# A two-block transformer kernel on one core: identity first, flips and weights in turn, small vectors between the weights, a few products on a cleared tile

## The chip, the cores and the metric

The kernel runs on one core of a Trainium2 chip. The metric is the device time of one execution in microseconds (us). The engines are TensorE (PE in the profile, its weight loads PEld), VectorE (DVE), ScalarE (ACT), GpSimd (POOL) and SyncE (SP), which here only issues transfers. A transfer issued by SP or ACT runs on 16 DMA engines that all queues share.

## What is computed

The input x has 256 rows of 2048 numbers in fp32. A first block adds stick-breaking attention and a squared-ReLU MLP, a second block runs two layers of latent attention beside a gated depthwise convolution. Cut to what the start of the program touches:

```python
hn = rms_norm(x, norm_mix_g)
q, k, v = split(hn @ sb_w_qkv, 3)          # 2048 x 6144 weights: the first work of TensorE
q = rms_norm(q per head, q_g); k = rms_norm(k per head, k_g)
...                                         # attention, w_o, MLP of 8192
cos, sin = rope_tables(positions)           # second block
mod = silu(c) @ ada_w[l] + ada_b[l]         # shift, scale, gate
u = causal_depthwise_conv(u, dw_w[l], dw_b[l])   # 31 taps
```

## The kernel before, in words

All weights are streamed once from HBM. A **unit** is 256 rows of a weight matrix by up to 512 columns, 512 KB, and there are 648 of them. SP loads it into one of NR = 5 buffers of RAW. ScalarE rounds it to fp32r (WH, four buffers), VectorE subtracts to get the rest (WL), and TensorE then multiplies: for each of the two 128-row pieces and each half of x three products (high by high, high by low, low by high), 12 matmuls of 512 columns. A load may be issued when the unit five places earlier has left its buffer, that is when its WL is written (`w_low`).

The first eight units, 0 to 7, are the first 512 columns of the query weights and each needs two of the sixteen 128-column pieces of x turned over. That is `x_turn` i: four transposes on TensorE, two ACTIVATEs to AH on ScalarE (times the gain norm_mix_g), two subtractions to AL on VectorE. Unit i needs `x_turn` i and the x piece i // 2.

Every engine walks through the same list of steps, -1, 0, 1, ... Step n stands behind unit n on TensorE. In each step an engine first does the tasks filed under `after[n]` and then, on ScalarE and VectorE, converts the units filed under `split[n]`. Unit u is converted in step u - 4, so three units ahead of use; only the first few are earlier. Nothing is reordered: an engine that waits in its list holds all that stands behind.

```python
for i in range(3):
    after[-1].append(("x_turn", "qkv", i))
for i in range(3, 8):
    after[i - 3].append(("x_turn", "qkv", i))
...
after[6].append(("columns", 0))
```

The task `columns` turns small vectors into columns. They are gathered in VR by 14 transfers, with the convolution taps in DR (31 rows, 248 KB), the positions in PI and four copies of norm gains in TRG (`vload`, 20 transfers). SP issues these after the first five weights. On VectorE `columns` also copies the taps and computes the rotary angles, a chain of small operations. TensorE needs consts (CST, 400 KB, its first 128 columns are the identity) before it can turn anything. ACT issues that transfer, behind the gain.

Of the kernel before, what the change touches and what calls it, by code (L numbers as in the profile page):

```python
# [80 lines left out]
def build(nc, A, out):  # L81
    ctx = ExitStack()
    with ctx:
# [21 lines left out]
        FB = put("FB", [128, 4, 512])  # L105
# [73 lines left out]
        vload, col = [], {"norm_mix_g": VC[:, 0:16]}  # L179
# [12 lines left out]
        vload.append((DR[:, :, :], A["dw_w_2"].rearrange("l k c -> k l c"), {}))  # L192
        vload.append((PI[:, :], A["positions_2"].rearrange("a (t p) -> p (a t)", p=128), {"allow_slow_non_contiguous": True}))
        for l in range(2):
            vload.append((TRG[:, 2 * l, :], A["q_norm_g_2"][l:l + 1, 128:192].to_broadcast([128, 64]), {}))
            vload.append((TRG[:, 2 * l + 1, :], A["k_norm_g_2"][l:l + 1, 128:192].to_broadcast([128, 64]), {}))
# [198 lines left out]
        T = Banks(P, 4, [sem(f"bank_ready{i}") for i in range(4)], [sem(f"bank_emptied{i}") for i in range(4)])  # L395
        s_cst, s_gain, s_vec, s_bias, s_out = sem("consts_in"), sem("gain_in"), sem("vectors_in"), sem("bias_in"), sem("stored")
# [43 lines left out]
        def tensor_program(e):  # L440
# [17 lines left out]
            def columns(part):  # L458
                pb = bank(("columns", 0))
                e.wait_ge(s_vec, 16 * len(vload))  # L460
# [3 lines left out]
                m.then_inc(*T.filled(("columns", 0)))  # L464
                pb = bank(("columns", 1))
                for l in range(2):
# [165 lines left out]
            tasks = dict(x_turn=x_turn, columns=columns, ada_sum=ada_sum, qk_turn=qk_turn, sb_scores=sb_scores, sb_sums=sb_sums, sb_out=sb_out,  # L632
# [26 lines left out]
            for name, *a in after[-1]:  # L659
                if name in tasks:  # L660
                    tasks[name](*a)
# [27 lines left out]
        def scalar_program(e):  # L689
# [32 lines left out]
            def columns(part):  # L722
                e.wait_ge(*cols.at("rest"))
                e.activation(CC[:, :], col["c_2"], ACT.Silu).then_inc(*c_act.up(0))
# [260 lines left out]
            for step in range(-1, NU):  # L985
                for name, *a in after[step]:
                    if name in tasks:
                        tasks[name](*a)
                highs(step)

        def vector_program(e):
# [31 lines left out]
            def columns(part):  # L1023
# [7 lines left out]
                e.tensor_tensor(GQ[:, 1:3], col["q_norm_g_2"], col["k_norm_g_2"], ALU.mult).then_inc(*cols.up("gq"))  # L1031
                e.wait_ge(*T.ready(("columns", 1)))
                e.tensor_copy(DW[:, :, :, :].rearrange("p a b c -> p (a b c)"), T.ap(("columns", 1))[:, 0:496]).then_inc(*T.drained(("columns", 1)))
# [92 lines left out]
            def rope_tables(l):  # L1126
                e.wait_ge(*angle_a.at("cos"))
                e.wait_ge(s_vec, 16 * len(vload))
# [185 lines left out]
            tasks = dict(x_turn=x_turn, x_add=x_add, rms=rms, columns=columns, ada_sum=ada_sum, qk_norm=qk_norm, sb_scores=sb_scores, sb_sums=sb_sums,  # L1314
# [26 lines left out]

            e.wait_ge(*T.ready(("mix", 0)))
            e.tensor_copy(VC[:, 0:16], T.ap(("mix", 0))[:, 0:16]).then_inc(*T.drained(("mix", 0)))
            for step in range(-1, NU):
# [5 lines left out]
        def pool_program(e):  # L1350
# [60 lines left out]
            for step in range(-1, NU):  # L1411
# [4 lines left out]
        def sync_program(e):  # L1416
# [106 lines left out]
```

## Time and profile before

| | |
|---|---|
| runs of the kernel before, us | 1999.87, 2002.76, 2004.25 (median 2002.76) |
| the profiled execution, us | 1999.04 |
| its span, us | 1997.2 |
| granted TensorE clock, mean over the span | 0.992 |
| busy: PE, DVE, ACT, POOL | 98%, 75%, 51%, 6% |

The span is the time from the first to the last record of the profiled execution, 1.8 us less than its own time. A busy share is taken over the whole span. A matmul that waits for its operands is not busy, and one that runs at the lower clock is. The engines work side by side, so the shares don't add up.

### The profile page before, as it was taken

The page shows a single profiled execution, that of the slowest core. Times are in us where ns is not written, and L with a number is a line of the kernel's source. Part 1 is how long each engine was busy: PE and PEld are TensorE (multiplying, and loading weights), DVE is VectorE, ACT ScalarE, POOL GpSimd, SP SyncE. Part 2 cuts the span into 40 slices and gives each one's busy share as a digit, 9 for nine tenths or more (in the row PEclk, how much of TensorE's full clock was granted, in tenths as well). Part 3 has the DMA queues.
Part 4 walks back from the last instruction along what each step waited for, and adds up shares of the span by engine and source line. Part 5 has one row for each costly group of instructions (what it writes and reads, how often), then busy time and mean ns, then how long its engine had stood idle before and what let it go on. Part 6 is the DMA issues. An engine that isn't in the chain of part 4 may idle for free.

```text
span 1997.2 us, 24786 instructions
## 1 busy us (share of the span) xinstructions
PE 1950.3 (98%) x9260; PEld 1628.1 (82%) x9260; DVE 1499.6 (75%) x2013; ACT 1019.5 (51%) x1471; POOL 126.7 (6%) x86
## 2 busy tenths in 40 slices
PE   7999999999999999999999989999999899999998
PEld 5788888888888888888888878888877688888877
DVE  4787777777677777767775567988886778888865
ACT  5455455445444444453434454566645545667452
POOL 0222232000000000000000000101000000011000
PEclk9999999999999999999999999999999999999999
DMA  6776867788888888888886545654544466555444
GB/s 219 250 240 226 291 219 259 246 282 308 277 298 280 291 303 283 296 289 293 284 301 222 187 153 147 203 167 141 166 147 158 128 191 183 167 161 153 159 146 139
DMA packets 225167, 441.95 MB, mean 221 GB/s; under 512 B 15685, under 2 KB 56919, under 8 KB 225047
## 3 DMA queue, kind: packets, MB, share of 16 engines
q1 hardware_dynamic: 224867, 439.93, 68.0%
q8 instruction: 74, 1.21, 0.2%
q14 instruction: 46, 0.38, 0.1%
q10 hardware_dynamic: 180, 0.43, 0.1%
HBM read 438.20 MB, written 2.10 MB: 220 GB/s over the span
## 4 chain that ended last, share of the span: by engine, by line
PE 80%; DVE 6%; issue 6%; ACT 4%; POOL 3%; SPq 1%; DMA 1%; POOLq 0%; DVEq 0%; ACTq 0%
PE P L681 24%; PE P L683 24%; PE P L682 24%; PE P L449 2%; DVE WL L996 2%; POOL ST L1352 2%; DVE CA L993 1%; PE P L477 1%; POOL QK L1374 1%; SPq L1448 1%; ACT WH L980 1%; PE P L554 1%; DMA RAW<-in_sb_w_qkv_dram 1%; PE P L564 0%; PE P L565 0%
## 5 line engine op out<-in xcount | busy, mean ns | idle before, releaser
L996 DVE TENSOR_TENSOR WL<-RAW,WH 128x1024 fp32r<-128x1024 f32 x648 | 790.4, 1225 | 340.5 <-ACT WH L980 339.0
L980 ACT ACTIVATE WH<-RAW 128x1024 fp32r<-128x1024 f32 x648 | 670.8, 1045 | 596.2 <-PE P L683 464.8
L681 PE MATMUL P<-WH,AH 128*128 128x512 f32 (+1 forms) x1536 | 604.7, 394 | 8.1 <-DVE WL L996 5.7
L683 PE MATMUL P<-WH,AL 128*128 128x512 f32 (+1 forms) x1536 | 595.3, 388 | 0.0
L682 PE MATMUL P<-WL,AH 128*128 128x512 f32 (+1 forms) x1536 | 594.4, 387 | 0.0
L681 PE MATMUL P<-WH,BH 128*128 128x512 f32 x896 | 355.8, 397 | 0.0
L682 PE MATMUL P<-WL,BH 128*128 128x512 f32 x896 | 351.2, 392 | 0.0
L683 PE MATMUL P<-WH,BL 128*128 128x512 f32 x896 | 351.2, 392 | 0.0
L681 PEld LDWEIGHTS P<-WH,AH 128*128 128x128 f32 x1536 | 289.4, 188 | 65.9 <-issue 4.9
L683 PEld LDWEIGHTS P<-WH,AL 128*128 128x128 f32 x1536 | 289.3, 188 | 59.1
L682 PEld LDWEIGHTS P<-WL,AH 128*128 128x128 f32 x1536 | 289.7, 189 | 55.5
L993 DVE SCALAR_TENSOR_TENSOR ADA<-RAW,CC,ADA 128x1024 f32<-128x1024 f32 x180 | 238.3, 1324 | 0.0
L993 DVE SCALAR_TENSOR_TENSOR CA<-UT,DW,CA 128x256 f32<-128x256 f32 x480 | 204.3, 477 | 0.0
L683 PEld LDWEIGHTS P<-WH,BL 128*128 128x128 f32 x896 | 169.8, 189 | 36.2
L682 PEld LDWEIGHTS P<-WL,BH 128*128 128x128 f32 x896 | 169.9, 190 | 34.3
L681 PEld LDWEIGHTS P<-WH,BH 128*128 128x128 f32 x896 | 169.6, 189 | 34.1
L1352 POOL TENSOR_TENSOR ST<-ST,CST 128x4 f32<-128x4 f32 (+2 forms) x34 | 62.8, 1846 | 1584.2 <-DVE ST L1021 943.2
L1013 DVE TENSOR_TENSOR X<-X,P 128x512 f32<-128x512 f32 x72 | 46.2, 682 | 8.6 <-PE P L683 8.6
L996 DVE TENSOR_TENSOR BL<-FB,BH 128x512 fp32r<-128x512 f32 x32 | 22.2, 692 | 26.0 <-ACT BH L802 26.0
L698 ACT ACTIVATE JX<-X 128x512 f32<-128x512 f32 x32 | 20.2, 631 | 39.4 <-DVE X L1013 21.9
L798 ACT ACTIVATE FB<-P 128x512 f32<-128x512 f32 x32 | 19.2, 599 | 29.6 <-PE P L449 29.6
L996 DVE TENSOR_TENSOR BL<-P,BH 128x512 fp32r<-128x512 f32 x24 | 16.5, 688 | 20.0 <-ACT BH L964 13.9
(242 smaller groups left out, 1407.6 us busy)
## 6 DMA issues: line engine op xcount, KB each, us to landing
RAW<-in_ada_w_dram SPq DMA_DIRECT2D x192, 512.0 KB, 4.9
RAW<-in_mlp_w_in_dram SPq DMA_DIRECT2D x128, 512.0 KB, 4.5
RAW<-in_mlp_w_out_dram SPq DMA_DIRECT2D x128, 512.0 KB, 5.2
RAW<-in_sb_w_qkv_dram SPq DMA_DIRECT2D x96, 512.0 KB, 4.7
RAW<-in_w_in_dram SPq DMA_DIRECT2D x80, 512.0 KB, 3.8
RAW<-in_w_in_dram SPq DMA_DIRECT2D x128, 256.0 KB, 3.2
RAW<-in_w_out_dram SPq DMA_DIRECT2D x64, 512.0 KB, 3.7
RAW<-in_sb_w_o_dram SPq DMA_DIRECT2D x32, 512.0 KB, 5.6
```

The lines of the kernel that those rows point to most:

```text
L449: m = e.transpose(pb[:, (2 * i + t) * 128:(2 * i + t + 1) * 128], src[:, t, kt * 128:(kt + 1) * 128], IDN)
L477: m = e.matmul(pb[:, j:j + 1], ACC2[:, slot, j * 128:(j + 1) * 128], ONE[:, 0:1], start=True, stop=True)
L554: m = e.transpose(pb[0:n, (2 * h + t) * 128:(2 * h + t + 1) * 128], src, IDN)
L681: e.matmul(o, xh, wh, start=st and k == 0, stop=False)
L682: e.matmul(o, xh, wl, start=False, stop=False)
L683: m = e.matmul(o, xl, wh, start=False, stop=u.last and k == u.nk - 1)
L698: e.activation(scratch, x, ACT.Square, scale=scale, accum_out=total).then_inc(*tally.up(*name))
L980: e.activation(WH[:, n % NH, 0:size], RAW[:, i % NR, 0:size], ACT.Copy).then_inc(w_high, 1)
L993: return e.scalar_tensor_tensor(out=o, in0=x, scalar=s, in1=y, op0=op0, op1=op1)
L996: return e.tensor_tensor(o, x, h.bitcast(F32), ALU.subtract)
L1013: m = e.tensor_tensor(o, o, psum(g, c, t), ALU.add)
L1352: return e.tensor_tensor(o, x, MH.to_broadcast([128, n]), ALU.pow)
```

## The change

It does five things. (1) ACT issues the identity alone (128 columns) first, then the gain, then the other 673 columns of consts, with a semaphore for each. (2) There is a step -2: `x_turn` i moves from step i - 3 to step i - 2 (0 to -2, 1 to -1, 2 to 0), and units 0 and 1 are converted in steps -2 and -1, one behind each turn. (3) The 14 transfers to VR are issued in pairs behind loads 5 to 11, and the other six (`late`) one by one behind loads 12 to 17. (4) `columns` moves from step 6 to step 9; the taps and the angles become a task of their own, `taps`, in step 20, and ScalarE's sines move from steps 9 and 10 to steps 21 and 22. (5) VectorE clears 256 columns of FB, and TensorE runs four fp32 products on them ahead of everything else.

```diff
+        after[20].append(("taps",))
...
-            step = -1 if u < 2 else 0 if u < 4 else u - 4
+            step = u - 2 if u < 3 else max(u - 4, 0)
...
-        for i in range(3):
-            after[-1].append(("x_turn", "qkv", i))
-        for i in range(3, 8):
-            after[i - 3].append(("x_turn", "qkv", i))
+        for i in range(8):
+            after[i - 2].append(("x_turn", "qkv", i))
...
-        after[6].append(("columns", 0))
-        after[9].append(("angles", 0))
-        after[10].append(("angles", 1))
+        after[9].append(("columns",))
+        after[20].append(("taps",))
+        after[21].append(("angles", 0))
+        after[22].append(("angles", 1))
...
+            e.wait_ge(warm, 1)
+            for i in range(4):
+                e.matmul(P[:, 3, 0:256], FB[:, 0, 0:128], FB[:, 0, 0:256], start=True, stop=True)
             e.wait_ge(s_gain, 16)
-            e.wait_ge(s_cst, 16)
+            e.wait_ge(s_idn, 16)
...
+            e.dma_start(CST[:, 0:128], A["consts"][:, 0:128]).then_inc(s_idn, 16)
             e.dma_start(VR[0:16, 0, :], A["norm_mix_g"].rearrange("a (r p) -> (a r) p", p=128)).then_inc(s_gain, 16)
-            e.dma_start(CST[:, :], A["consts"]).then_inc(s_cst, 16)
+            e.dma_start(CST[:, 128:801], A["consts"][:, 128:801]).then_inc(s_cst, 16)
...
             load(4)
-            for dst, src, k in vload:
-                e.dma_start(dst, src, **k).then_inc(s_vec, 16)
             for i in range(5, len(items)):
                 load(i)
+                if i < 12:
+                    for dst, src, k in vload[2 * i - 10:2 * i - 8]:
+                        e.dma_start(dst, src, **k).then_inc(s_vec, 16)
+                elif i < 12 + len(late):
+                    dst, src, k = late[i - 12]
+                    e.dma_start(dst, src, **k).then_inc(s_late, 16)
```

ScalarE's list from the gain to unit 5, before (AH is a turned piece of x, WH a converted unit, x2 two of the same in a row, JX,ST the sums of squares):

```order
L709 ACTIVATE AH<-P,VC 128x256 x6
L980 ACTIVATE WH<-RAW 128x1024 x2
L709 ACTIVATE AH<-P,VC 128x256 x2
L980 ACTIVATE WH<-RAW 128x1024 x3
L709 ACTIVATE AH<-P,VC 128x256 x2
L980 ACTIVATE WH<-RAW 128x1024
```

and of the change:

```order
L716 ACTIVATE AH<-P,VC 128x256 x2
L987 ACTIVATE WH<-RAW 128x1024
L716 ACTIVATE AH<-P,VC 128x256 x2
L987 ACTIVATE WH<-RAW 128x1024
L716 ACTIVATE AH<-P,VC 128x256 x2
L987 ACTIVATE WH<-RAW 128x1024 x3
L716 ACTIVATE AH<-P,VC 128x256 x2
L987 ACTIVATE WH<-RAW 128x1024
```

The first unit's WH now stands behind one turned pair and no longer behind three; each later turn stands one step nearer to the unit that needs it.

SP's list behind the x pieces and weights 0 to 4, before, first and last of the 20 small transfers:

```order
L1448 DMA VR<-in_norm_mlp_g_dram 16x128
L1448 DMA VR<-in_norm_g_dram 32x128
...
L1448 DMA VR<-in_ada_b_dram 96x128
L1448 DMA DR<-in_dw_w_dram 31x2x1024
L1448 DMA PI<-in_positions_dram 128x2x1
L1448 DMA TRG<-in_q_norm_g_dram 128x64
...
L1441 DMA RAW<-in_sb_w_qkv_dram 128x2x512 x12
```

and of the change, loads 11 to 15:

```order
L1453 DMA RAW<-in_sb_w_qkv_dram 128x2x512
L1463 DMA VR<-in_c_dram 16x128
L1463 DMA VR<-in_ada_b_dram 96x128
L1453 DMA RAW<-in_sb_w_qkv_dram 128x2x512
L1466 DMA DR<-in_dw_w_dram 31x2x1024
L1453 DMA RAW<-in_sb_w_qkv_dram 128x2x512
L1466 DMA PI<-in_positions_dram 128x2x1
L1453 DMA RAW<-in_sb_w_qkv_dram 128x2x512
L1466 DMA TRG<-in_q_norm_g_dram 128x64
```

The block of small transfers that stood between loads 4 and 5 is gone; the taps now stand between loads 12 and 13.

## Rows read from the trace of the kernel before

**Rows 1.** Windows: length, then PE, PEld, DVE, ACT, POOL busy us, granted clock, DMA
```profile
200.00:1000.00 800.00, 798.50 (x3746) 665.28 (x3745) 596.59 (x570) 375.95 (x445) 44.89 (x29) 1.00 0.84 281
```
**Rows 2.** Timeline of PE: the taps' turns, starts of units 8, 9, 10, 11
```profile
41.85 1.18 PE L469 MATMUL P<-CST,DR 31*128 31x31 f32 x16
...
45.81 0.39 PE L681 MATMUL P<-WH,AH 128*128 128x512 f32 x1
...
48.53 0.39 PE L681 MATMUL P<-WH,AH 128*128 128x512 f32 x1
...
53.22 0.50 PE L681 MATMUL P<-WH,AH 128*128 128x512 f32 x1 [1.81 <-DVE WL L996]
...
57.66 0.40 PE L681 MATMUL P<-WH,AH 128*128 128x512 f32 x1
```
**Rows 3.** Timeline of PE behind unit 0: turn 3, then unit 1
```profile
19.22 0.95 PE L449 MATMUL P<-CST,X 128*128 128x128 f32 x4
19.93 0.48 PE L681 MATMUL P<-WH,AH 128*128 128x512 f32 x1
```
**Rows 4.** Timeline of the start: start us, length us, engine, line, [idle before <-releaser]
```profile
7.67 0.25 PE L658 MATMUL P<-CST,VR 16*128 16x16 f32 x1 [7.67 <-DMA CST<-in_consts_dram]
...
9.08 2.54 ACT L709 ACTIVATE AH<-P,VC 128x256 fp32r<-128x256 f32 x6 [6.07 <-PE P L449]
...
11.51 2.00 ACT L980 ACTIVATE WH<-RAW 128x1024 fp32r<-128x1024 f32 x2
...
13.96 0.76 PE L681 MATMUL P<-WH,AH 128*128 128x512 f32 x1 [3.28 <-DVE WL L996]
```
**Rows 5.** Timeline of ACT and PE: weights 5 and 6 converted, units 5 and 6 start
```profile
32.15 1.06 ACT L980 ACTIVATE WH<-RAW 128x1024 fp32r<-128x1024 f32 x1 [7.47 <-DMA RAW<-in_sb_w_qkv_dram]
...
35.21 1.04 ACT L980 ACTIVATE WH<-RAW 128x1024 fp32r<-128x1024 f32 x1
...
35.31 0.50 PE L681 MATMUL P<-WH,AH 128*128 128x512 f32 x1 [2.00 <-DVE AL L993]
...
38.35 0.50 PE L681 MATMUL P<-WH,AH 128*128 128x512 f32 x1
```
**Rows 6.** Timeline of DVE: taps copied, three steps of the angles, units 10 and 11
```profile
46.54 0.67 DVE L1033 COPY DW<-P 128x496 f32<-128x496 f32 x1
...
48.56 2.40 DVE L993 SCALAR_TENSOR_TENSOR AG<-AG 128x64 f32<-128x64 f32 x3
...
51.94 2.36 DVE L996 TENSOR_TENSOR WL<-RAW,WH 128x1024 fp32r<-128x1024 f32 x2
```
**Rows 7.** Transfers, issue to landing in us: x piece 0, weight 0, weight 4
```profile
X<-in_x_dram SPq DMA_DIRECT2D x1, 512.0 KB, 4.4
RAW<-in_sb_w_qkv_dram SPq DMA_DIRECT2D x1, 512.0 KB, 6.3
RAW<-in_sb_w_qkv_dram SPq DMA_DIRECT2D x1, 512.0 KB, 11.6
```
**Rows 8.** The chain of waits, SP's issues of the same three; then weight 5's flight
```profile
0.74 0.43 SPq L1444
1.23 0.47 SPq L1441
...
5.58 0.53 SPq L1441
...
21.15 10.98 DMA RAW<-in_sb_w_qkv_dram
```
**Rows 9.** The page: line, engine, operation, tiles, count | busy us, mean ns | idle before
```profile
L993 DVE SCALAR_TENSOR_TENSOR ADA<-RAW,CC,ADA 128x1024 f32<-128x1024 f32 x180 | 238.3, 1324 | 0.0
```
**Rows 10.** Timeline of PE: an fp32 product of 256 columns (two records), the next one
```profile
97.92 0.59 PE L493 MATMUL P<-QT 128*128 128x256 f32 x2
98.35 0.38 PE L494 MATMUL P<-QT 128*128 128x128 f32 x2
```
**Rows 11.** Windows: the queue between weight 4 and weight 5 (columns as in rows 1)
```profile
17.00:21.00 4.00, 4.00 (x15) 3.14 (x14) 0.00 (x0) 0.73 (x3) 0.00 (x0) 1.00 0.15 35
```

More of the change, by code:

```diff
@@ L191, in build @@
                 nrow[g] = r + n
[L192 to L193 removed]
+        late.append((DR[:, :, :], A["dw_w_2"].rearrange("l k c -> k l c"), {}))
+        late.append((PI[:, :], A["positions_2"].rearrange("a (t p) -> p (a t)", p=128), {"allow_slow_non_contiguous": True}))
         for l in range(2):
[L195 to L196 removed]
+            late.append((TRG[:, 2 * l, :], A["q_norm_g_2"][l:l + 1, 128:192].to_broadcast([128, 64]), {}))
+            late.append((TRG[:, 2 * l + 1, :], A["k_norm_g_2"][l:l + 1, 128:192].to_broadcast([128, 64]), {}))
         of = lambda name, n, l: col[name][:, n * l:n * l + n]
@@ L456, in x_turn, with columns @@
                 turn(pb, X, 1, 2 * i + 1).then_inc(*T.filled(("x_turn", g, i)))
-            def columns(part):
+            def columns():
                 pb = bank(("columns", 0))
+                e.wait_ge(s_cst, 16)
                 e.wait_ge(s_vec, 16 * len(vload))
@@ L464, in columns, with taps @@
                 m.then_inc(*T.filled(("columns", 0)))
+            def taps():
                 pb = bank(("columns", 1))
+                e.wait_ge(s_late, 16 * len(late))
                 for l in range(2):
@@ L630, in p_turn @@
                 turn(pb, MP, 1, 2 * i + 1).then_inc(*T.filled(("pt2", l, c, i)))
-            tasks = dict(x_turn=x_turn, columns=columns, ada_sum=ada_sum, qk_turn=qk_turn, sb_scores=sb_scores, sb_sums=sb_sums, sb_out=sb_out,
+            tasks = dict(x_turn=x_turn, columns=columns, taps=taps, ada_sum=ada_sum, qk_turn=qk_turn, sb_scores=sb_scores, sb_sums=sb_sums, sb_out=sb_out,
                          hid_turn=hid_turn, h_turn=h_turn, glu=glu, lat_turn=lat_turn, att_turn=att_turn, att_scores=att_scores,
@@ L653, in await_rows @@
                     e.wait_ge(*T.emptied(("pt2", g[1], (k - 8) // 4, k // 2 % 2)))
+            e.wait_ge(warm, 1)
+            for i in range(4):
+                e.matmul(P[:, 3, 0:256], FB[:, 0, 0:128], FB[:, 0, 0:256], start=True, stop=True)
             e.wait_ge(s_gain, 16)
-            e.wait_ge(s_cst, 16)
+            e.wait_ge(s_idn, 16)
             pb = bank(("mix", 0))
             e.transpose(pb[:, 0:16], VR[0:16, 0, :], CST[0:16, 0:16]).then_inc(*T.filled(("mix", 0)))
-            for name, *a in after[-1]:
+            for name, *a in after[-2] + after[-1]:
                 if name in tasks:
@@ L720, in x_square, with columns @@
                     square_sum(JX[:, t, :], X[:, t, c * 512:(c + 1) * 512], ST[:, 64 + 4 * t + c:65 + 4 * t + c], sq_sum, g, c, t)
-            def columns(part):
+            def columns():
                 e.wait_ge(*cols.at("rest"))
@@ L980, in highs @@
                         e.activation(WH[:, n % NH, 0:size], RAW[:, i % NR, 0:size], ACT.Copy).then_inc(w_high, 1)
+            e.dma_start(CST[:, 0:128], A["consts"][:, 0:128]).then_inc(s_idn, 16)
             e.dma_start(VR[0:16, 0, :], A["norm_mix_g"].rearrange("a (r p) -> (a r) p", p=128)).then_inc(s_gain, 16)
-            e.dma_start(CST[:, :], A["consts"]).then_inc(s_cst, 16)
+            e.dma_start(CST[:, 128:801], A["consts"][:, 128:801]).then_inc(s_cst, 16)
             e.preload_act_table_set("silu_and_others")
-            for step in range(-1, NU):
+            for step in range(-2, NU):
                 for name, *a in after[step]:
@@ L1021, in rms, with columns @@
                 e.tensor_scalar(ST[:, 72:74], ST[:, 72:74], 1.0 / D, EPS, ALU.mult, ALU.add).then_inc(*ms.up(g))
-            def columns(part):
+            def columns():
                 e.wait_ge(*T.ready(("columns", 0)))
@@ L1031, in columns, with taps @@
                 e.tensor_tensor(GQ[:, 1:3], col["q_norm_g_2"], col["k_norm_g_2"], ALU.mult).then_inc(*cols.up("gq"))
+            def taps():
                 e.wait_ge(*T.ready(("columns", 1)))
+                e.wait_ge(s_cst, 16)
                 e.tensor_copy(DW[:, :, :, :].rearrange("p a b c -> p (a b c)"), T.ap(("columns", 1))[:, 0:496]).then_inc(*T.drained(("columns", 1)))
@@ L1127, in rope_tables @@
                 e.wait_ge(*angle_a.at("cos"))
-                e.wait_ge(s_vec, 16 * len(vload))
+                e.wait_ge(s_late, 16 * len(late))
                 if l:
@@ L1312, in o_add @@
                     e.tensor_tensor(o, o, FB[:, t, :], ALU.add).then_inc(*(x_done if part else x_mid).up(l, c, t))
-            tasks = dict(x_turn=x_turn, x_add=x_add, rms=rms, columns=columns, ada_sum=ada_sum, qk_norm=qk_norm, sb_scores=sb_scores, sb_sums=sb_sums,
+            tasks = dict(x_turn=x_turn, x_add=x_add, rms=rms, columns=columns, taps=taps, ada_sum=ada_sum, qk_norm=qk_norm, sb_scores=sb_scores, sb_sums=sb_sums,
                          sb_out=sb_out, hid_turn=hid_turn, mod_scale=mod_scale, x_norm=x_norm, h_turn=h_turn, h_low=h_low_, pads=pads_, rope_tables=rope_tables,
@@ L1340, in lows @@
                             fma(acc, r, CC[:, kt:kt + 1], acc, ALU.mult, ALU.add).then_inc(ada_used, 1)
+            e.memset(FB[:, 0, 0:256], 0.0).then_inc(warm, 1)
             e.wait_ge(*T.ready(("mix", 0)))
             e.tensor_copy(VC[:, 0:16], T.ap(("mix", 0))[:, 0:16]).then_inc(*T.drained(("mix", 0)))
-            for step in range(-1, NU):
+            for step in range(-2, NU):
                 for name, *a in after[step]:
@@ L1410, in pool_program @@
             e.wait_ge(s_cst, 16)
-            for step in range(-1, NU):
+            for step in range(-2, NU):
                 for name, *a in after[step]:
```

3 lines of the change are left out of this document (2 added, 1 removed).

## The prediction, as it was put on record before the result

> **What bounds the kernel now.** I read the page first: TensorE is busy for 98% of the span, the others for 75% and less (the table above). The windows then say where its idle time lies. In a stretch of 800 us in the middle TensorE is busy 798.5 [rows 1], so a weight that arrives earlier there is worth nothing, and what TensorE lacks at the start is carried to the end: whatever brings its steady part forward by 1 us shortens the program by about 1 us. The change touches the first 22 steps only, so I followed TensorE from unit to unit up to the 12th. A unit costs 2.72 us where nothing holds it (45.81 to 48.53 [rows 2]), a turn of x 0.7 (19.22 to 19.93 [rows 3]). Against that TensorE loses five pieces:
>
> - It waits for the consts until 7.67, and unit 0 starts at 13.96 [rows 4].
> - Unit 0 takes 5.26 us (13.96 to 19.22 [rows 3, 4]), twice its price. So its matmuls stand 0.44 us apart, at 1.2 GHz, where those of unit 8 stand 0.23 apart, at 2.4 GHz: 2.5 us lost.
> - 2.0 us ahead of unit 5. TensorE waits for AL, which stands on ScalarE and VectorE behind weight 5, and ScalarE had waited 7.47 us for that transfer [rows 5].
> - 1.8 us ahead of unit 10, whose WL VectorE writes only after taps and angles: the chain runs from 46.54 to 51.94, 5.4 us [rows 2, 6].
> - Unit 10 takes 4.44 us (53.22 to 57.66 [rows 2]): the clock fell behind that pause, 1.7 us lost.
>
> **The change part by part.**
>
> *Identity first, one turn and one unit in turn.* x piece 0 is issued at 0.74 and lands 4.4 later, at 5.1; weight 0 is issued at 1.23 and lands 6.3 later, at 7.5 [rows 7, 8]. The bytes ahead of them stay the same but for the order on ACT's queue. The identity alone is not in the trace. It is 64 KB of the 400, issued 0.5 us earlier than consts were, so it can't land after consts did (7.5) and hardly after x piece 0; I take 5.1 for the first transpose. From TensorE's first product to ScalarE's first AH were 1.4 us (7.67 to 9.08), and six AH took 2.54, so two take 0.85 [rows 4]: AH 0 ends at 5.1 + 1.4 + 0.85 = 7.4. Then WH 0 can start when weight 0 is there, 7.5, where it was 11.51. From WH 0 to unit 0 were 2.45 us [rows 4]; unit 0 starts at about 9.95, **4.0 us earlier**. Bounds: if the identity came no earlier than consts, WH 0 would start at 9.9, and 2.4 of the 4.0 would go; nothing lets unit 0 start before weight 0 has landed, so there is no gain beyond 4.0 but the few tenths by which that landing may move. Turn 2, done before unit 0 until now, comes behind it: **0.7 us later**. Does one unit of lead suffice for a turn? ScalarE's round of AH, two sums of squares and WH takes 3.06 us (32.15 to 35.21 [rows 5]), a unit with its turn 3.4 on TensorE, and AL is needed a full unit after the transposes. So it does; in the first steps WH 3 and WH 4 wait for weight 4 (5.58 + 11.6 = 17.2 [rows 7, 8]) ahead of turn 3, and I find 0 to 0.3 us for unit 3.
>
> *Small vectors behind the loads.* Weight 5 was issued at 21.15 and landed 10.98 later, at 32.13 [rows 8], although its buffer was free once WL 0 was written, before unit 0 began at 13.96 [rows 4]. Now it is issued at about 9.9, directly behind weight 4, and lands about 1.2 us behind 17.2 (eight transfers of this size landed from 7.5 to 17.2). ScalarE no longer waits for it, and the pause ahead of unit 5 goes: **2.0 us**.
>
> *Taps and angles in step 20.* The 16 turns of the taps (1.1 us on TensorE) are only moved. VectorE has only the copies of the small vectors in step 9, so the pause ahead of unit 10 goes, **1.8 us**, and with it the low clock in unit 10, **1.7 us**. What hid nothing in step 6 is hidden in step 20: behind unit 20 VectorE has the turns (1.1), the chain (at most 5.4), one accumulation (1.3 [rows 9]) and WL 24 (1.2 [rows 6]), 9.0 us; unit 24 starts 1.1 + 3 x 2.72 = 9.3 us behind unit 20. If that cover fails, the price is the rival below.
>
> *Products on a cleared tile.* Such a product takes 0.43 us at 2.4 GHz (97.92 to 98.35 [rows 10]), so 0.86 at 1.2, and four 3.4 us. They start when SP and ACT start, near 1, end at about 4.5, before x piece 0 is there, and cost nothing by themselves. Do they raise the clock for unit 0? TensorE then works from 1 to 7 but for half a microsecond, pauses from about 7 to 9.95, and begins unit 0. The trace has three cases to weigh that by: 5.3 us of unit 0 in a row went by before the clock rose; a pause of 1.8 us ahead of unit 10 was followed by low clock; one of 2.0 ahead of unit 5 was not (unit 5 took 3.04 us, 35.31 to 38.35) [rows 2, 5]. The pause of 2.9 us is longer than both, so I take it that unit 0 is in large part slow again and gain only **0.4 us** of 2.5. Bounds: nothing, and all 2.5. The Trainium skill ("TensorE: Matmul & The Clock Gate", section "What's actually happening") says that the throttled clock is the default and that activity releases it; the trace agrees for unit 0. By that rule alone the products would give the 2.1 us that I leave out, which is the second case below.
>
> **The sum:** 4.0 - 0.7 + 0.4 + 2.0 + 1.8 + 1.7 = 9.2 us. The profiled execution was 1999.04 us and would be 1989.8. The median of the runs is 3.7 us above it, 2002.76, and the forecast for such a median is 1993.5 us.
>
> **The rivals.**
>
> *The clock stays up through the pause.* Unit 0 costs 2.72. Gain 9.2 + 2.1 - 0.2 (unit 3 then waits for weight 4) = 11.1, time 1991.7.
>
> *The taps hold the weights back.* This is where the small transfers can still bite. Between the landing of weight 4 and of weight 5 lay 14.9 us (17.2 to 32.1 [rows 7, 8]), though from 17 to 21 the 16 DMA engines were busy to a share of 0.15 and moved 35 GB/s [rows 11]: that is the work of two or three of them, and a weight's share on these would have to wait. The Trainium skill ("DMA: Bandwidth & Descriptors", section "Why a DMA increments its semaphore by 16 and not by 1") gives a reason: a transfer is split over the largest number up to 16 that divides its slowest dimension, so 31 rows go over one engine. The trace, with two or three engines' work, roughly agrees. In the changed kernel that transfer stands ahead of weight 13. Counted from the end of unit 3: weight 12 is issued after the turn, AH, squares, WH and WL of step 3, 5.1 us; it lands 4.4 later, weight 13 at most 14.9 after that, at 24.4, and with WH and WL it is ready at 26.8. Unit 13 starts after nine units and three turns, 26.6, plus the turns of vectors and queries that I leave out. So it is just in time even by the upper bound. If the hold is 3 us longer, unit 13 waits some 3 us and the clock falls behind it (1.7): gain 4.5, time 1998.3.
>
> *The angle chain is not hidden in step 20,* because accumulations pile up there: a pause of 1 to 2 us ahead of unit 24 and 1.7 for the clock. Gain 5.9, time 1996.9.
>
> *The start does not move*: the identity, x piece 0 and weight 0 share the DMA engines with the rest of the consts, and unit 0 starts near 12.3. Gain 9.2 - 2.4 = 6.8, time 1996.
>
> *Slower than before.* The same hold as in the second rival, but repeated: positions and the four copies of gains now stand behind a load each, and if each of the six holds the queue as long as the taps' share of the 14.9, units 13 to 17 starve. With the clock's 1.7 it decides where the total hold is 7.5 us above the 14.9 (9.2 - 1.7), and the price grows one for one from there; 12 us more give 2007.3. Against it: in the trace all twenty together made 14.9.
>
> **How the numbers follow.** Forecast 0.48 (own range 1991 to 1995.5), clock up 0.22, taps 0.10, angles 0.07, start unmoved 0.09, slower 0.04. The runs of before lie 4.4 us apart, and 0.2%, 4 us, is about what a measurement of this kernel tells from no change. The first two cases give faster; of the three middle ones, at 4.5 to 6.8 us, a third may be measured within 4: faster 0.87, same 0.09, slower 0.04. The range reaches from the clock case less 2 us of scatter, 1989.5, to the taps case, 1998.5.
>
> **What the profile after would show.** First transposes near 5; unit 0 at 9.5 to 10.5; its 12 matmuls 0.43 apart if I am right on the clock, 0.23 if not; no pause ahead of unit 5 or 10; unit 10 in 2.72; unit 11 near 47.4 where it was 57.66 (9.2 and the moved 1.1); no pause of TensorE at units 13 to 17 nor at 24; the windows from 200 on as before. A start of unit 0 behind 11, a pause at unit 13, or steady stretches that are longer than before would make me wrong.

## The result, and the profile after

| | kernel before | changed kernel |
|---|---|---|
| median of six runs each, us | 2001.16 | 1992.09 |
| lowest to highest, us | 1999.27 to 2004.25 | 1987.08 to 1993.42 |
| the profiled execution, us | 1999.04 | 1991.99 |
| ratio of the times | | 0.9949, 95% interval 0.9935 to 0.9964 |

The changed kernel is 9.1 us faster by the medians and 10.2 by the ratio; the forecast was 9.2, at 1993.5 us. The total came out nearly as worked out, but several of its terms did not, and 3.5 us of it were booked under a step that, as the runs show, was not needed for them. The forecast of 1993.5 was worked out from a median of before of 2002.76; over six runs that median is 2001.16, so 9.2 us less would now be 1992.0.

TensorE's first 20 us in the changed kernel, timeline rows that answer to [rows 3, 4]:

```profile
1.19 3.78 PE L661 MATMUL P<-FB 128*128 128x256 f32 x8 [1.19 <-DVE FB L1353]
6.14 0.28 PE L665 MATMUL P<-CST,VR 16*128 16x16 f32 x1 [1.17 <-DMA VR<-in_norm_mix_g_dram]
6.36 1.97 PE L449 MATMUL P<-CST,X 128*128 128x128 f32 x8
10.76 0.77 PE L688 MATMUL P<-WH,AH 128*128 128x512 f32 x1 [2.44 <-DVE WL L1004]
11.32 0.63 PE L689 MATMUL P<-WL,AH 128*128 128x512 f32 x1
...
16.02 0.60 PE L449 MATMUL P<-CST,X 128*128 128x128 f32 x4
16.38 0.48 PE L688 MATMUL P<-WH,AH 128*128 128x512 f32 x1
...
19.91 0.47 PE L688 MATMUL P<-WH,AH 128*128 128x512 f32 x1
```

Unit 0 starts at 10.76 and not at 9.95, and what the first product on data from memory (L665) waited for is in its brackets: the gain, not x. The chain of waits has that transfer as its longest early piece (start, length):

```profile
0.74 0.45 ACTq L989
1.22 4.88 DMA VR<-in_norm_mix_g_dram
6.14 0.28 PE P L665
```

Unit 0 still takes 5.26 us (10.76 to 16.02), its matmuls 0.43 us apart, 1.2 GHz; those of unit 1 stand 0.23 apart.

I then read off where each unit starts on TensorE in either trace (the starts are those of timeline rows as above; the last row is the difference):

```
unit             0      1      2      3      4      5      6      7      9     10     11     12
before       13.96  19.93  23.46  26.66  29.87  35.31  38.35  42.95  48.53  53.22  57.66  61.21
after        10.76  16.38  19.91  23.08  26.28  29.49  32.69  35.54  40.98  44.18  47.02  50.53
gained        3.20   3.55   3.55   3.58   3.59   5.82   5.66   7.41   7.55   9.04  10.64  10.68
```

The gain has four steps: the start, the pause ahead of unit 5, the work moved out from ahead of unit 7 (lent, since it returns in step 20), and unit 10 with the pause ahead of it. From unit 12 on nothing changes until the taps' turns, 1.17 us at 76.45 in the changed kernel, take their part back. To compare kernels behind all of this I use one **mark**: the start of ScalarE's last pair of scaled evictions of query and key columns. It stands at 308.29 before, and in the changed kernel here:

```profile
299.03 0.69 ACT L747 ACTIVATE QK<-P,ST 128x512 f32<-128x512 f32 x1 [1.60 <-PE P L690]
```

That is 9.26 us earlier. The expectations of runs a to h speak of a later mark, VectorE's first addition to x (380.54 before, 371.25 in the changed kernel); the table behind the runs has both. The windows of the steady part (columns as in [rows 1]) are as they were, 798.50 us busy of 800:

```profile
200.00:1000.00 800.00, 798.50 (x3747) 665.32 (x3746) 598.42 (x574) 374.53 (x442) 43.00 (x28) 1.00 0.84 281
```

One term of the second rival can be read as well. ScalarE's timeline between units 10 and 12 (with the wait in brackets), and below it the issue and flight of weight 13, which stands behind the taps:

```profile
48.80 1.06 ACT L987 ACTIVATE WH<-RAW 128x1024 fp32r<-128x1024 f32 x1 [2.59 <-DMA RAW<-in_sb_w_qkv_dram]
50.17 1.06 ACT L987 ACTIVATE WH<-RAW 128x1024 fp32r<-128x1024 f32 x1 [0.31 <-DMA RAW<-in_sb_w_qkv_dram]
```
```profile
RAW<-in_sb_w_qkv_dram SPq DMA_DIRECT2D x1, 512.0 KB, 14.5
```
```profile
31.48 0.33 SPq L1466 DMA_DIRECT2D DR<-in_dw_w_dram  x1
34.27 0.39 SPq L1453 DMA_DIRECT2D RAW<-in_sb_w_qkv_dram  x1
```

Weight 13 takes 14.5 us from its issue to its landing, where the six weights before it took 3.8 to 6.6. It lands at 48.8, 13.5 us behind weight 12 (issued at 31.06, 4.2 us to landing); the bound that I took for that distance was 14.9. The hold that I feared is there nearly in full. ScalarE waits 2.59 us for it, and TensorE nothing: WL of unit 13 is written from 49.89 to about 51.2, and unit 13 starts at 53.37, so some 2 us of cover are left.

### The profile page after: what moved, and what is told of

Read it like the earlier page. It is cut to its first block, busy times and chain, and to the rows that moved or that the text cites. A ratio compares the mean times of both kernels' runs of the same rounds, so it can differ in the third digit from the quotient of the medians.

```text
span 1990.2 us, 24805 instructions
## 1 busy us (share of the span) xinstructions
PE 1953.2 (98%) x9268; PEld 1630.4 (82%) x9268; DVE 1498.4 (75%) x2014; ACT 1019.5 (51%) x1471; POOL 126.0 (6%) x86
## 4 chain that ended last, share of the span: by engine, by line
PE 82%; DVE 6%; issue 6%; ACT 4%; POOL 3%; DMA 0%; POOLq 0%; DVEq 0%; ACTq 0%
PE P L688 25%; PE P L690 25%; PE P L689 25%; PE P L449 2%; DVE WL L1004 2%; POOL ST L1364 2%; DVE CA L1001 1%; PE P L481 1%; POOL QK L1386 1%; ACT WH L987 1%; PE P L558 1%; PE P L568 0%; PE P L569 0%; ACT FB L705 0%; DVE FB L1262 0%
```

## The experiments

Each is told against the kernel before or the changed kernel, whichever its diff starts from. The table at the end of this section has their times and marks.

**a_order: the new order and the identity alone, small vectors as before.** From the kernel before:

```diff
-            step = -1 if u < 2 else 0 if u < 4 else u - 4
+            step = u - 2 if u < 3 else max(u - 4, 0)
...
-        for i in range(3):
-            after[-1].append(("x_turn", "qkv", i))
-        for i in range(3, 8):
-            after[i - 3].append(("x_turn", "qkv", i))
+        for i in range(8):
+            after[i - 2].append(("x_turn", "qkv", i))
...
+            e.dma_start(CST[:, 0:128], A["consts"][:, 0:128]).then_inc(s_idn, 16)
...
-            e.dma_start(CST[:, :], A["consts"]).then_inc(s_cst, 16)
+            e.dma_start(CST[:, 128:801], A["consts"][:, 128:801]).then_inc(s_cst, 16)
...
```

> The kernel before with the start order alone: identity first, x_turn i in step i - 2, units 0 and 1 converted one behind each turn. The vectors still stand between loads 4 and 5, columns with taps and angles in step 6. No cleared-tile products. Mark: the start of VectorE's first addition of x (380.5 us before, 371.3 after the whole change). If each piece of the sum stood for itself, this part would give 3.2 - 0.7 us: mark near 378. My theory is that it can't: weight 5 still lands near 32, and turn 4 now stands behind WH 5 on ScalarE, so that unit 4, which before started at 29.87, waits as well, until about 35.3. Then unit 5 starts near 38.5 instead of 35.3, and the mark is 383 to 386 (3.2 us later, up to 1.7 more if the clock falls in the longer pause). The whole kernel would be 2 to 6 us slower than before.

It is slower than the kernel before, by 3.8 us at the mark, though unit 0 starts at 10.14. The timelines of ScalarE and TensorE around unit 4:

```profile
32.35 1.06 ACT L980 ACTIVATE WH<-RAW 128x1024 fp32r<-128x1024 f32 x1 [12.85 <-DMA RAW<-in_sb_w_qkv_dram]
33.31 0.82 ACT L709 ACTIVATE AH<-P,VC 128x256 fp32r<-128x256 f32 x2
```
```profile
35.50 0.79 PE L681 MATMUL P<-WH,AH 128*128 128x512 f32 x1 [10.57 <-DVE AL L994]
36.09 0.63 PE L682 MATMUL P<-WL,AH 128*128 128x512 f32 x1
...
64.20 1.09 PE L448 MATMUL P<-CST,QK 128*128 128x128 f32 x8 [1.50 <-POOL QK L1376]
```

Weight 5 comes as late as before (32.35 against 32.15 [rows 5]), and in the new order the turn that unit 4 needs stands behind it on ScalarE, no longer the one that unit 5 needs. So TensorE stops one unit earlier, for 10.57 us, and what it gained at the start it spends waiting. It comes back at the low clock (0.43 us between matmuls until 40.4), and unit 5 starts at 41.02, 5.7 us later than before. Part of that comes back: this kernel has no pause ahead of unit 10 and no low clock in it, so unit 11 starts at 59.81, only 2.2 us later than before. Then a new pause of 1.50 us, in which TensorE waits for GpSimd (last row above), brings it to the 3.8 at the mark.

**b_vectors: the small vectors, taps and angles alone, start as before.** From the changed kernel: order of turns, consts in one transfer and no products, as before the change.

> The whole change without its start: consts in one transfer behind the gain, three turns ahead of unit 0, no products. Only the vectors between the weights, columns in step 9, taps in step 20. If the pieces add up: pause ahead of unit 5 gone (2.0), pause ahead of unit 10 gone (1.8 to 2.0) and unit 10 at full clock (1.7), with unit 6's wait and the restarts (about 0.8): mark near 374.2. Rival: the start matters more than I booked and the vectors less: mark at 377 or later. Unit 0 at 13.96 as before, at 1.2 GHz.

It is 7.7 us earlier at the mark, of the 9.3 of the whole change, with no pause ahead of units 5 and 10. Some 0.85 us of that are luck of the clock: its unit 0 takes 4.41 us and not 5.26, at a start (13.81) and behind a pause (3.29) like those of the kernel before. Its rows:

```profile
13.81 0.48 PE L687 MATMUL P<-WH,AH 128*128 128x512 f32 x1 [3.29 <-DVE WL L1002]
14.12 0.60 PE L688 MATMUL P<-WL,AH 128*128 128x512 f32 x1
14.52 0.63 PE L689 MATMUL P<-WH,AL 128*128 128x512 f32 x1
...
17.50 0.41 PE L687 MATMUL P<-WH,AH 128*128 128x512 f32 x1
17.76 0.40 PE L688 MATMUL P<-WL,AH 128*128 128x512 f32 x1
```

It begins at 2.4 GHz, falls within the second matmul and is up again from 17.5.

a and b are not additive: -3.8 and +7.7 make 3.9, together they give 9.3. In these runs the order pays only where weight 5 comes in time.

**c_no_products: the changed kernel without the four products.**

```diff
-            e.wait_ge(warm, 1)
-            for i in range(4):
-                e.matmul(P[:, 3, 0:256], FB[:, 0, 0:128], FB[:, 0, 0:256], start=True, stop=True)
...
-            e.memset(FB[:, 0, 0:256], 0.0).then_inc(warm, 1)
```

> The whole change without the cleared tile and the four products. Theory: they buy nothing, since unit 0 ran at 1.2 GHz with them: unit 0 near 10.76, 5.26 us long, unit 1 at full clock, mark 371.3 within 0.3. Rival: they shorten the low stretch, and without them unit 1 is slow as well: unit 1 takes up to 5.3 us, mark up to 2.5 us later, 373.8.

Unit 0 takes 4.24 us, less than with them, and starts at 10.04, since the gain's transfer happened to land in 4.2 us and not in 4.9. At the mark this kernel is 1.8 us ahead of the changed one, at the later mark of the expectation 0.2 (371.03 against 371.25), and the intervals of the ratios (0.9963 and 0.9949) overlap. No gain of the four products is seen.

**d_gain_first: the gain ahead of the identity.**

```diff
-            e.dma_start(CST[:, 0:128], A["consts"][:, 0:128]).then_inc(s_idn, 16)
             e.dma_start(VR[0:16, 0, :], A["norm_mix_g"].rearrange("a (r p) -> (a r) p", p=128)).then_inc(s_gain, 16)
+            e.dma_start(CST[:, 0:128], A["consts"][:, 0:128]).then_inc(s_idn, 16)
```

> The whole change with ACT's first two transfers swapped: gain first, then the identity. In the changed kernel the first transpose waited for the gain (8 KB, issued at 1.22 behind the identity, landed at 6.1; before, issued at 0.73, it took 2.9). Theory: the gain lands near 3.7 and the identity near 5.4, x piece 0 near 5.4: first transposes near 5.5, unit 0 0.5 to 0.7 us earlier (10.1 to 10.3), mark 370.7. Rival: whichever of the two comes second takes 4.9 us: first transposes at 6.1 and no change, mark 371.3.

My theory fell: the start is later, 11.44. The transfers issued from 0.5 to 1.6 (size, issue to landing in us):

```profile
CST<-in_consts_dram ACTq DMA_DIRECT2D x1, 64.0 KB, 5.5
VR<-in_norm_mix_g_dram ACTq DMA_DIRECT2D x1, 8.0 KB, 3.1
```

The gain is there after 3.1 us, but the identity, now second, takes 5.5. In the changed kernel it is 4.2 for the identity as the first and 4.9 for the gain as the second. Whichever stands second on ACT's queue is late. The later mark is at 372.36, where I had expected 370.7.

**e_bridge: three more products between turn 1 and unit 0.** In the changed kernel, behind the loop that turns x:

```diff
+            for i in range(3):
+                e.matmul(P[:, 3, 0:256], FB[:, 0, 0:128], FB[:, 0, 0:256], start=True, stop=True)
```

> The whole change with three more fp32 products on the cleared tile between turn 1 and unit 0. In the changed kernel TensorE paused there for 2.4 us (from 8.3 to 10.76), and unit 0 ran at 1.2 GHz throughout. Theory: what keeps unit 0 slow is that pause; with it filled (three products are 2.6 us at 1.2 GHz, 1.3 at 2.4) unit 0 takes 2.7 to 3.5 us instead of 5.26, and the mark (VectorE's first addition of x, 371.3) moves to 369 to 369.6. Rival: TensorE's work before unit 0 is too little whatever stands in the pause: unit 0 takes 4 to 5.3 us as in the earlier runs and starts 0.2 us later, mark 370.5 to 371.5.

They fill the pause that the changed kernel has from about 8.3 to 10.76, and unit 0 runs at 2.4 GHz from its first matmul, in 2.84 us. The mark is 2.4 us ahead of the changed kernel's:

```profile
7.61 2.41 PE L670 MATMUL P<-FB 128*128 128x256 f32 x6
10.26 0.47 PE L690 MATMUL P<-WH,AH 128*128 128x512 f32 x1 [0.24 <-DVE WL L1006]
10.56 0.40 PE L691 MATMUL P<-WL,AH 128*128 128x512 f32 x1
10.80 0.40 PE L692 MATMUL P<-WH,AL 128*128 128x512 f32 x1
...
13.10 0.60 PE L449 MATMUL P<-CST,X 128*128 128x128 f32 x4
```

At the later mark only 0.9 us of this is left: 370.38, where the expectation had 369 to 369.6 and the changed kernel has 371.25. In between lies a stretch in which this kernel's clock was low and the changed kernel's was not; first this kernel, then the changed one:

```profile
320.00:340.00 20.00, 19.91 (x112) 17.25 (x111) 14.97 (x20) 12.42 (x22) 7.67 (x8) 0.93 0.57 199
```
```profile
320.00:340.00 20.00, 19.92 (x117) 17.44 (x116) 15.09 (x21) 13.41 (x23) 6.83 (x8) 1.00 0.63 228
```

So what the bridge does to unit 0 is shown, and that the whole kernel keeps all of it is not.

**f_taps_split: the kernel before, only the taps' transfer cut into 16 and 15 rows.**

```diff
-        vload.append((DR[:, :, :], A["dw_w_2"].rearrange("l k c -> k l c"), {}))
+        taps_in = A["dw_w_2"].rearrange("l k c -> k l c")
+        vload.append((DR[0:16, :, :], taps_in[0:16], {}))
+        vload.append((DR[16:31, :, :], taps_in[16:31], {}))
```

> The kernel before, with the taps' transfer in two: rows 0 to 15 and rows 16 to 30, nothing else. It tests why weight 5 landed 14.9 us behind weight 4. Theory, the Trainium skill's rule (a transfer goes over the largest number up to 16 that divides its slowest dimension): 31 rows are on one DMA engine, 254 KB at 1/16 of the rate; 16 and 15 rows go over 16 and 15. SP then isn't held up by the last four small transfers, weight 5 is issued near 16 to 17 instead of 21.15 and lands near 21 to 23; the pause ahead of unit 5 goes, and unit 10 may still wait for the angles: mark 376 to 378 instead of 380.5, whole kernel 2 to 5 us faster than before. Rival: the 20 small transfers cost by their number: weight 5 lands within 2 us of 32, no change.

Two transfers in place of one give 5.85 us at the mark. SP issues weight 5 at 16.88 and it is there 5.7 us later, at 22.6, where the kernel before has 32.1 [rows 8]. Of these 9.5 us, 4.3 come from the issue: behind the 31 rows SP took 1.2 to 2.1 us for each of the four copies of gains, and here 0.43 to 0.47. The other 5.3 come from the flight, 10.98 us before. The two rows on the queue:

```profile
16.88 11.00 SPq L1443 DMA_DIRECT2D RAW<-in_sb_w_qkv_dram  x6
```
```profile
RAW<-in_sb_w_qkv_dram SPq DMA_DIRECT2D x1, 512.0 KB, 5.7
```

There is no pause ahead of unit 5, and none ahead of unit 10, although taps and angles are still in step 6. VectorE does the chain from 40.77 on, and its three multiply-adds, 2.40 us in the kernel before [rows 6], take 0.75. Its rows, GpSimd's product of the first query columns, and the start of unit 10:

```profile
40.77 0.67 DVE L1035 COPY DW<-P 128x496 f32<-128x496 f32 x1
...
42.78 0.75 DVE L995 SCALAR_TENSOR_TENSOR AG<-AG 128x64 f32<-128x64 f32 x3
...
44.52 4.06 DVE L998 TENSOR_TENSOR WL<-RAW,WH 128x1024 fp32r<-128x1024 f32 x2
```
```profile
45.71 2.87 DVE L998 TENSOR_TENSOR WL<-RAW,WH 128x1024 fp32r<-128x1024 f32 x1
```
```profile
44.80 2.69 POOL L1368 TENSOR_TENSOR SQ<-QK 128x1024 f32<-128x1024 f32 x1 [5.54 <-ACT QK L743]
```
```profile
48.64 0.39 PE L683 MATMUL P<-WH,AH 128*128 128x512 f32 x1
```

In the kernel before the same product fell into the chain (shortest, median and longest of the three multiply-adds in ns, then first and last start):

```profile
48.99 1.89 POOL L1366 TENSOR_TENSOR SQ<-QK 128x1024 f32<-128x1024 f32 x1 [3.94 <-ACT QK L741]
```
```profile
L993 DVE SCALAR_TENSOR_TENSOR AG<-AG x3: 224/225/1885, 48.6 to 49.1; 128x64 f32<-128x64 f32 x3
```

The third multiply-add began 0.1 us behind the product and ended 0.1 us behind it, 1.65 us longer than the other two. Here the product runs beside unit 11's WL instead (the second of the pair, 2.87 us and not 1.22), behind the chain and behind unit 10's WL.

**l_split_moved: f, and columns in step 9, taps and angles in steps 20 to 22.** Same split as f, plus the change's own task and steps.

> The kernel before with the taps' transfer in 16 and 15 rows, and columns in step 9, taps in step 20, angles in 21 and 22 as in the change; the vectors still ahead of load 5. With the split alone the mark (last eviction of query columns) stood at 302.44, and TensorE had no pause ahead of unit 10 although the angles were still in step 6. If the move out of step 6 is worth the 3.5 us that I booked for it (1.8 of pause and 1.7 of clock), the mark is 299. Theory now: that pause was a late result of weight 5, VectorE running one unit behind, and the move is worth no more than 0.3 to 0.7 us once the weights come in time: mark 301.7 to 302.2, give or take 0.9 for how long unit 0 stays slow (I compare that apart).

The mark moves from 302.44 to 302.17, and half of that is there at unit 1 already (19.76 against 19.91), ahead of all that was moved. So with the hold gone the move is worth 0.3 us at most, and not the 1.8 + 1.7 that I had put down to it. No run has the move while weight 5 is still late, so what it would be worth there is not shown.

**g_mix_late: the changed kernel, TensorE turns x before it waits for the gain.** The wait and the gain's own turn stand behind turn 0:

```diff
+            e.wait_ge(s_idn, 16)
+            for name, *a in after[-2]:
+                if name in tasks:
+                    tasks[name](*a)
             e.wait_ge(s_gain, 16)
-            e.wait_ge(s_idn, 16)
             pb = bank(("mix", 0))
...
-            for name, *a in after[-2] + after[-1]:
+            for name, *a in after[-1]:
```

> The whole change with the gain's own turn moved behind turn 0 on TensorE. In the changed kernel the first transpose of x waited for the gain, which landed at 6.1, though x piece 0 was there at 5.4 and the identity at 4.9. Theory: first transposes at 5.4 to 5.5, first AH at about 6.9 instead of 7.57 (gain column copied right behind turn 0), unit 0 0.4 to 0.7 us earlier, 10.1 to 10.3; mark 370.6 to 370.9. Rival: the landings shift by as much from execution to execution as is gained (the gain took 4.2 to 4.9 us in three runs): nothing to see.

The first transposes now start at 5.64, and their bracket names x; unit 0 starts at 9.87, 0.9 earlier and about where the prediction had it (9.95), and takes 5.26 as before. At either mark 0.5 us is left of it.

```profile
5.64 0.63 PE L449 MATMUL P<-CST,X 128*128 128x128 f32 x4 [0.68 <-DMA X<-in_x_dram]
```

**h_all: g, the bridge of e, and the late taps cut in 16 and 15 rows.**

> The whole change with all three edits: the gain's turn behind turn 0, three products between turn 1 and unit 0, the taps' transfer in 16 and 15 rows. In the changed kernel ScalarE waited 2.6 us for weight 13, behind the taps, without harm to TensorE. Theory: this wait goes (weight 13 lands at most 6 us after its issue instead of 14.5), TensorE is as it was there; unit 0 as in the two runs with the single edits; mark 368.3 to 369 if the bridge works, 370.5 if it doesn't. Over the whole kernel 2 to 3 us, or 1 us, below the change, which the scatter of the end may hide.

Weight 13 lands in time (ScalarE waits for no transfer from 26 to 60 us, where the changed kernel's waits there come to 4.6), unit 0 takes 2.81 us at 2.4 GHz, and the mark is at 297.10, 11.2 ahead of before (the later one at 369.36, a little behind the 368.3 to 369 expected). One wait is new: unit 3 for AL.

```profile
20.46 0.50 PE L695 MATMUL P<-WH,AH 128*128 128x512 f32 x1 [0.45 <-DVE AL L1008]
```

**j_turn_first: h, unit 4 converted one step later, behind turn 3.**

```diff
-            step = u - 2 if u < 3 else max(u - 4, 0)
+            step = u - 2 if u < 3 else 0 if u == 3 else max(u - 4, 1)
```

> The kernel with all three edits (gain's turn late, bridge of three products, taps in 16 and 15 rows), and unit 4 converted in step 1 behind turn 3 rather than in step 0 ahead of it. There TensorE waited 0.45 us for turn 3's AL, which stood behind weight 4. Theory: this wait goes, nothing else moves: mark 296.6 (297.10 without the edit). Rival: weight 4 is then converted later and unit 4 or 5 waits: mark 297.1 or later. Whole kernel equal to it within 1 us, 13 us below before.

The wait at unit 3 is gone, and unit 3 starts 0.5 us earlier. The mark is 1.2 us earlier, more than that wait can give, and at the later mark this kernel is 0.4 us behind h, so no gain beyond the wait is shown. Turn and unit 3:

```profile
19.58 0.60 PE L451 MATMUL P<-CST,X 128*128 128x128 f32 x4
19.93 0.48 PE L695 MATMUL P<-WH,AH 128*128 128x512 f32 x1
```

**i_bridge_only: e without the first four products.**

> The whole change without the four products at the very start, but with three between turn 1 and unit 0. With both (seven products) unit 0 ran at 2.4 GHz from its first matmul; with the four alone it took 5.26 us, with none 4.2. Theory: the first four matter to nothing by themselves, but with the bridge TensorE needs their work to have the clock up by unit 0: without them unit 0 is still slow in part, 3.5 to 5 us. Rival: the bridge alone does it: unit 0 takes 2.8 us. Mark from here on: ScalarE's eviction of the last query columns (QK<-P,ST; 308.29 before, 299.03 after the change, 296.63 with seven products, 297.23 with none): 297 to 298.5 by the theory, 296.6 by the rival.

The bridge alone does it:

```profile
7.60 2.77 PE L668 MATMUL P<-FB 128*128 128x256 f32 x6
10.25 0.76 PE L688 MATMUL P<-WH,AH 128*128 128x512 f32 x1
10.81 0.56 PE L689 MATMUL P<-WL,AH 128*128 128x512 f32 x1
11.21 0.40 PE L690 MATMUL P<-WH,AL 128*128 128x512 f32 x1
```

The bridge products begin at 1.2 GHz here (2.77 us for the three, 2.41 in e, 1.46 in h), and the clock is up from the third matmul of unit 0, which takes 3.25 us. The rival was right, and the theory that the first four are needed fell.

All in one table (medians in us, of before beside it on the same chip; "earlier" is against the marks of before, 308.29 and, for the later one, 380.54):

```
                  median  before   ratio   95% interval    unit 0 starts, takes   mark    earlier   later mark  earlier
changed kernel   1992.09 2001.16  0.9949  0.9935-0.9964      10.76    5.26      299.03    9.26     371.25    9.29
a_order          2002.93 1999.53  1.0021  1.0010-1.0032      10.14    4.26      312.13   -3.84     384.33   -3.79
b_vectors        1994.82 1999.53  0.9969  0.9959-0.9980      13.81    4.41      300.62    7.67     372.82    7.72
c_no_products    1992.65 1999.53  0.9963  0.9949-0.9976      10.04    4.24      297.23   11.06     371.03    9.51
d_gain_first     1991.61 1999.53  0.9961  0.9946-0.9976      11.44    5.26      300.15    8.14     372.36    8.18
e_bridge         1989.43 2001.43  0.9936  0.9921-0.9950      10.26    2.84      296.63   11.66     370.38   10.16
f_taps_split     1996.31 2001.43  0.9963  0.9950-0.9977      14.01    5.26      302.44    5.85     374.63    5.91
g_mix_late       1991.35 2001.43  0.9940  0.9922-0.9958       9.87    5.26      298.54    9.75     370.77    9.77
h_all            1987.92 2001.43  0.9930  0.9915-0.9944       9.88    2.81      297.10   11.19     369.36   11.18
i_bridge_only    1987.62 2002.58  0.9924  0.9907-0.9940      10.25    3.25      296.52   11.77     368.74   11.80
l_split_moved    1995.56 2002.58  0.9960  0.9946-0.9975      14.02    5.25      302.17    6.12     374.41    6.13
j_turn_first     1987.90 2002.58  0.9928  0.9913-0.9943      10.01    2.84      295.93   12.36     369.76   10.78
```

The order of the marks is finer than what the times can tell: i, j, h and e are one group by their intervals, 12 to 15 us faster than before by the medians. Each mark is from one execution, and low-clock stretches fall differently in each. Between the two marks c, e and j lose 1.5 to 1.6 us in such a stretch and the other kernels nothing, so c and e, 1.8 and 2.4 us ahead of the changed kernel at the first mark, are 0.2 and 0.9 ahead at the second. Differences of marks under 2 us carry little where the two marks don't agree.

## Why the prediction came out right, and where it was not

The ledger at unit 12 and beyond, by the terms of the sum:

```
term of the sum                    predicted   measured
start of unit 0                          4.0        3.2
the turn moved behind unit 0            -0.7       +0.2
clock in unit 0                          0.4        0.0
pause ahead of unit 5                    2.0        2.2
pause ahead of unit 10                   1.8        2.0
clock in unit 10                         1.7        1.6
columns and taps, moved                  0.0        0.1
sum                                      9.2        9.3
```

- **The start.** The mechanism was right: the identity alone came early (4.9), weight 0 no longer stood behind three turns. I looked at the identity, x piece 0 and weight 0 and left out the fourth transfer that the first product needs, the gain, which the change moves to second place; it landed at 6.1, a microsecond behind the 5.1 that I took. g shows that this wait was worth 0.9 us at unit 0. The other three terms of the start held: in g unit 0 starts at 9.87.
- **The moved turn.** I priced a turn at 0.7 from one row [rows 3]. The timelines have both prices: a turn between two units costs 0.35 in most places (26.31 to 26.66 before, 16.02 to 16.38 after) and 0.7 in some. The five turns that stood between units before cost 2.7 us in sum, the six of after 2.5. The start and this term were off by 0.8 and 0.9 in opposite directions, so the sum hid both. That is luck.
- **The clock in unit 0.** I gave it 0.4 and named 0.43 us between the matmuls as the sign. That sign came. But the reason that I gave, the length of the pause, is only half of it: c and a have the same pause, no products ahead of it and a shorter low stretch. e, h, i and j, where no pause of more than 1.6 us is left ahead of unit 0, are the only kernels in which it runs at 2.4 GHz all or nearly all the way. The rule of the Trainium skill that I set against the row ("TensorE: Matmul & The Clock Gate", section "What's actually happening"), activity releases the throttle, agrees with these four; the four early products released nothing that was still there at unit 0, behind pauses of 1.2 and 2.4 us.
- **The pause ahead of unit 5.** Size and place right (2.0, and 0.2 that unit 5 itself lost behind it, 3.04 us against 2.84). The cause was half named: I wrote that weight 5 stood behind the small transfers, and only in a rival that it is the taps' 31 rows. f shows that the rows alone are it. The Trainium skill ("DMA: Bandwidth & Descriptors", section "Why a DMA increments its semaphore by 16 and not by 1") says that a transfer goes over the largest number of engines up to 16 that divides its slowest dimension: one for 31 rows, 16 and 15 for the halves. By it the 16 engines that I named for every transfer, in the text ahead of the prediction, are an upper bound. The runs agree: 14.9 and 13.5 us between two landings with 31 rows in between. In f the weight behind the halves lands 5.7 us after its issue, and in h, where each half stands behind a weight of its own, the next two weights take 4.2 and 3.9.
- **Unit 10.** The move to step 20 is the step that failed as an explanation: f shows the 3.5 us gained without it, and l that it adds 0.3 at most. In the kernel before three things met. The chain stood in step 6. VectorE was late with it behind weight 5: it copies the taps 3.6 us behind the start of unit 7 (46.54 and 42.95), in f 0.4 behind (40.77 and 40.35). And 1.65 of the 5.4 us that I read as the chain's price were the multiply-add beside GpSimd's product; in step 20 of the changed kernel the whole chain takes 3.8 us (77.66 to 81.42). In f unit 10's WL is written by 45.75 and unit 10 starts at 48.64, 2.9 us of cover. The 3.2 us of lateness and the 1.65 eat that up and leave 1.9, about the pause of 1.8. The lateness alone would leave 0.3 of it, the 1.65 alone nothing (an estimate from these rows). In a weight 5 is as late, but TensorE has stopped for it as well, and there is no pause ahead of unit 10. So three terms of my sum, 5.5 us, come with one repair, and f alone measures it at 5.85.
- **The rivals.** The hold by the taps is confirmed as a mechanism (13.5 us for the 14.9 taken as its bound) and stayed hidden as worked out: unit 13 starts 2.2 us behind its WL. That it would repeat and add up at each small transfer is refuted: of the weights behind 13 each took less from issue to landing than the one before it, 12.7, 11.7, 10.1 and 8.3 us, as behind one hold that drains. Angles in step 20 made no pause of TensorE, and the clock was up in unit 0 only in e, h, i and j, by the bridge. That rival was priced at 1.9 us over the forecast; at the first mark e is 2.4 ahead of the changed kernel, at the later one 0.9.
- **The end.** In the profiled pair the gain is 9.3 us up to about 1150, and 7.0 at the end. It falls by 1.1 around 1185 and by 2.0 between 1485 and 1525, and comes back by 0.7 behind that. Both programs have a pause near the second place and low clock behind it, a little longer in the changed kernel: over the same 70 us of work (9.3 us earlier there) it was granted 0.93 and the kernel before 0.95. Such stretches differ from one execution to the next (the six runs of either kernel lie 5 and 6 us apart), so the medians, at 9.1, are the better measure. The changed kernel, then before:

```profile
1470.70:1540.70 70.00, 66.65 (x274) 51.80 (x273) 45.86 (x50) 34.90 (x46) 1.60 (x1) 0.93 0.46 150
```
```profile
1480.00:1550.00 70.00, 66.99 (x282) 52.39 (x282) 46.85 (x51) 36.72 (x47) 1.61 (x1) 0.95 0.45 148
```

- **The signs.** The first transposes started at 6.36 and unit 0 at 10.76, both later than the ranges that I gave. The 0.43 us in unit 0, no pause ahead of units 5, 10, 13 to 17 and 24, unit 11 at 47.02 and steady stretches as before all came.

What stays open: why unit 0 takes 5.26 us in the changed kernel, d and g (four early products) and in before, f and l (none), but 4.24 and 4.26 in c and a and 4.41 in b (none either). The pauses ahead of it are alike (2.4 to 3.3 us), and no run varied the point in time alone.

## What to carry to other kernels

Where a queue is slow and the DMA engines are nearly idle, look for one transfer like the 31 rows here before moving the work around it: the same rows as 16 and 15 were worth 5.85 us at the mark and 5.1 by the medians, more than half of the whole change. When a stage starts late, list every transfer that its first instruction needs; the smallest one, 8 KB, was what it waited for. To have the first real matmuls at 2.4 GHz, fill the pause directly ahead of them, and not the time long before. When several pauses follow one another in one list, look for one late arrival behind all of them before adding them up as separate repairs. And compare kernels at more than one mark: a stretch of low clock between two marks moved the order here.

## What the runs showed of the hardware

- A transfer of 8 KB as the second on ACT's queue, with x and weights starting beside it, took 4.2 to 5.1 us to land in eight kernels (4.9 in the changed one), and 2.7 to 3.2 as the first in five; the identity, 64 KB, took 3.2 to 4.5 as the first in eight and 5.5 as the second in one (d).
- The granted clock in the windows at the very start doesn't show the low clock that the spacing shows: the changed kernel's row reads 1.00 where matmuls stand 0.43 us apart. There the spacing is to be read.

```profile
12.00:16.00 4.00, 4.00 (x10) 2.94 (x10) 0.79 (x1) 0.00 (x0) 0.00 (x0) 1.00 1.05 387
```

- VectorE and GpSimd did not run side by side where GpSimd worked on 128x1024. A multiply-add of 0.23 us took 1.89 and ended 0.1 us behind GpSimd's product in the kernel before; in f a WL of 1.22 us took 2.87 and ended 1.1 us behind it, and the product, begun beside another WL, took 2.69 us and not 1.89.
